# Where the head norms' sums and spreads stand among the steps of two gated linear units

## The reference, cut to what matters

```python
o_a = _norm_f32(o_a) * jax.nn.silu(heads(rg))
o_b = _norm_f32(o_b) * gdn_norm_w * jax.nn.silu(heads(bg))
o_c = _norm_f32(o_c) * gla_norm_w * jax.nn.silu(heads(cg))
o_d = _norm_f32(o_d) * hgrn_norm_w * jax.nn.silu(heads(dg))
o = jnp.concatenate([o_a, o_b, o_c, o_d], axis=-1)
return jnp.matmul(o, w_out)

def _norm_f32(x):
    return x * lax.rsqrt(jnp.mean(x * x, axis=-1, keepdims=True) + EPS)
```

## Time and profile before

| | |
|---|---|
| median of three runs | 2418.09 us |
| the profiled execution | 2420.88 us, of which its span is 2419.1 us |
| mean granted TensorE clock | 0.973 of full |
| busy share of TensorE, VectorE, ScalarE, POOL | 97%, 68%, 27%, 8% |
| uses 15 to 28 of the mixers | about 324 to 368 us of the span |

### The profile page before, as it was taken

The page is one execution under the profiler, slowest core; times in us unless marked ns, Lnnn a source line. Parts: engine busy times, 40 slices in busy tenths (PEclk is TensorE's granted clock), DMA queues, the critical chain, the costliest instruction groups (busy, mean ns, idle before and its releaser), DMA issues.

```text
span 2419.1 us, 35289 instructions
## 1 busy us (share of the span) xinstructions
PE 2335.3 (97%) x14624; PEld 1898.2 (78%) x14624; DVE 1651.3 (68%) x2569; ACT 663.9 (27%) x1200; POOL 183.2 (8%) x179
## 2 busy tenths in 40 slices
PE   8998879999999999999989999999999999999997
PEld 6886668878888888887756788888888888888886
DVE  6674366756888865559788777666667886666653
ACT  2321253022211201324768413222102113222200
POOL 0001222001000011003211010000010000000000
PEclk9999579999999999999999999999999999999998
DMA  4220003412222453322200361232562451322341
GB/s 183 79 79 2 21 3 122 158 52 88 96 96 96 135 204 130 107 81 92 88 1 2 138 219 62 98 100 97 197 214 104 182 186 63 102 96 96 127 141 64
DMA packets 71728, 253.94 MB, mean 105 GB/s; under 512 B 8560, under 2 KB 8848, under 8 KB 71056
## 3 DMA queue, kind: packets, MB, share of 16 engines
q1 hardware_dynamic: 71280, 251.14, 30.4%
q10 hardware_dynamic: 288, 0.54, 0.1%
HBM read 247.97 MB, written 2.10 MB: 103 GB/s over the span
## 4 chain that ended last, share of the span: by engine, by line
PE 47%; DVE 3%; issue 0%; ACT 0%; POOL 0%; DVEq 0%; POOLq 0%
PE psum L393 14%; PE psum L394 14%; PE psum L395 13%; PE psum L3362 1%; PE psum L487 1%; PE psum L3349 1%; PE psum L3384 1%; DVE scratch L3440 1%; DVE scratch L3416 1%; PE psum L656 0%; PE psum L3376 0%; PE psum L465 0%; DVE h L534 0%; DVE n L530 0%; PE psum L476 0%
## 5 line engine op out<-in xcount | busy, mean ns | idle before, releaser
L393 PE MATMUL psum<-rounded_n,rounded_high 128*128 128x512 f32 x1824 | 722.1, 396 | 8.0 <-DVE rounded_ring L346 4.6
L394 PE MATMUL psum<-rounded_n_low,rounded_high 128*128 128x512 f32 x1824 | 712.1, 390 | 0.0
L395 PE MATMUL psum<-rounded_n,rounded_ring 128*128 128x512 f32 x1824 | 712.0, 390 | 0.0
L346 DVE TENSOR_TENSOR rounded_ring<-ring,rounded_high 128x1024 fp32r<-128x1024 f32 (+1 forms) x360 | 448.4, 1246 | 43.5 <-ACT rounded_high L329 31.5
L393 PEld LDWEIGHTS psum<-rounded_n,rounded_high 128*128 128x128 f32 x1824 | 343.9, 189 | 86.6 <-issue 7.4
L394 PEld LDWEIGHTS psum<-rounded_n_low,rounded_high 128*128 128x128 f32 x1824 | 344.1, 189 | 74.2 <-issue 3.9
L395 PEld LDWEIGHTS psum<-rounded_n,rounded_ring 128*128 128x128 f32 x1824 | 343.7, 188 | 72.1
L344 DVE CAST rounded_high<-ring 128x1024 fp32r<-128x1024 f32 (+1 forms) x347 | 250.4, 722 | 188.3 <-PE psum L395 177.9
L393 PE MATMUL psum<-rounded_arena,rounded_high 128*128 128x512 f32 x720 | 280.2, 389 | 0.0
L395 PE MATMUL psum<-rounded_arena,rounded_ring 128*128 128x512 f32 x720 | 280.1, 389 | 0.0
L394 PE MATMUL psum<-rounded_arena,rounded_high 128*128 128x512 f32 x720 | 280.1, 389 | 0.0
(11 more groups left out here) (507 smaller groups left out, 2798.3 us busy)
## 6 DMA issues: line engine op xcount, KB each, us to landing
ring<-in_w_up SPq DMA_DIRECT2D x132, 512.0 KB, 3.6
ring<-in_w_down SPq DMA_DIRECT2D x48, 512.0 KB, 3.5
n_low<-in_mod_w SPq DMA_DIRECT2D x48, 512.0 KB, 5.8
arena<-in_mod_w SPq DMA_DIRECT2D x48, 512.0 KB, 5.3
ring<-in_w_ab_in SPq DMA_DIRECT2D x37, 512.0 KB, 3.6
ring<-in_w_mix_in SPq DMA_DIRECT2D x31, 512.0 KB, 3.6
ring<-in_w_sc_in SPq DMA_DIRECT2D x24, 512.0 KB, 5.7
ring<-in_w_down SPq DMA_DIRECT2D x24, 384.0 KB, 3.0
```

What stands on the lines that cost most here:

```text
L346: nc.vector.tensor_tensor(self.rounded(raw), raw, self.rounded(high), ALU.subtract).then_inc(self.weights_split, 1)
L393: self.nc.tensor.matmul(out, w_high, x_high, start=first, stop=False)
L394: self.nc.tensor.matmul(out, w_high, x_low, start=False, stop=False)
L395: return self.nc.tensor.matmul(out, w_low, x_high, start=False, stop=last)
```

## The change

Sums, spreads, values, casts and low parts of tiles 0 to 5 are put at other places of the three hand-written lists. No instruction of them is added or dropped.

```diff
@@ TensorE @@
         use(14)
-        for i in range(4):
-            norm_sums(pe, i)
+        norm_sums(pe, 0)
         use(15)
+        norm_sums(pe, 1)
         use(16)
-        for i in range(3):
-            norm_spread(pe, i)
         use(17)
+        norm_sums(pe, 2)
         use(18)
-        norm_spread(pe, 3)
+        norm_sums(pe, 3)
         use(19)
         use(20)
-        for i in (4, 5):
-            norm_sums(pe, i)
+        norm_spread(pe, 0)
         use(21)
+        norm_spread(pe, 1)
         use(22)
+        norm_spread(pe, 2)
+        use(23)
+        norm_spread(pe, 3)
+        use(24)
+        norm_sums(pe, 4)
+        use(25)
+        norm_sums(pe, 5)
+        use(26)
+        use(27)
         for i in (4, 5):
             norm_spread(pe, i)
-        for x in range(23, len(uses)):
-            use(x)
+        use(28)
@@ ScalarE @@
-        norm_root(0)
-        after_use(15)
-        after_use(16)
+        for x in range(15, 19):
+            after_use(x)
         act.wait_ge(delta_kept, 2)
         for i in (4, 5):
             square(i)
-        after_use(17)
-        after_use(18)
-        for i in range(2):
+        norm_root(0)
+        for x in range(19, 22):
+            after_use(x)
+        high_part(0)
+        for i in (1, 2, 3):
+            after_use(21 + i)
             high_part(i)
-        after_use(19)
-        after_use(20)
-        for i in (2, 3):
-            high_part(i)
+        after_use(25)
+        after_use(26)
         norm_root(1)
-        for x in range(21, 25):
-            after_use(x)
+        after_use(27)
         for i in (4, 5):
             high_part(i)
-        for x in range(25, len(uses)):
-            after_use(x)
+        after_use(28)
@@ VectorE @@
         use(15)
-        norm_scale(0)
         use(16)
         k.split_until(dve, k.first_tile["mix_out"] + 1)
-        use(17)
-        norm_value(0)
-        norm_value(1)
-        use(18)
-        norm_value(2)
-        use(19)
-        norm_value(3)
-        low_part(0)
-        low_part(1)
+        for x in (17, 18, 19):
+            use(x)
+        norm_scale(0)
         use(20)
         dve.wait_ge(delta_kept, 2)
         for i in (4, 5):
             gate(i)
+        norm_value(0)
         use(21)
-        low_part(2)
-        low_part(3)
-        norm_scale(1)
+        norm_value(1)
         use(22)
         k.split_until(dve, k.first_tile["mix_out"] + 2)
+        low_part(0)
+        norm_value(2)
         use(23)
-        norm_value(4)
-        norm_value(5)
-        for x in range(24, 26):
-            use(x)
+        low_part(1)
+        norm_value(3)
+        use(24)
+        low_part(2)
+        use(25)
+        low_part(3)
+        use(26)
+        norm_scale(1)
+        use(27)
+        for i in (4, 5):
+            norm_value(i)
         for i in (4, 5):
             low_part(i)
-        for x in range(26, len(uses)):
-            use(x)
+        use(28)
```

## The result

The change makes the kernel slower. Six executions of the changed kernel have a median of 2429.53 us (2422.54 to 2431.47), six of the kernel before one of 2417.47 (2414.76 to 2421.79). The ratio is 1.0033 with a 95% interval of 1.0018 to 1.0049. A second set of eleven executions gave 1.0034 (1.0020 to 1.0049), so this is no accident of one set. The forecast was no change, 2420.8, with a range up to 2425.2; the result lies above it. The profiled execution took 2431.02 us with a span of 2429.2.

The account below looks back on a forecast made before the run. The prediction took the kernel as bound by TensorE (busy 97%), and the stage by when use 28 starts and how long it lasts. Terms -0.5 + 4.2 - 1.0 = +2.7 us on median 2418.09 gave 2420.8, range 2416.2 to 2425.2.

Parts of the forecast that it names:

- Part 1: End of unit 1: moving sums of tiles 1 to 3 from ahead of use 15 gains 2.6 to 3.2 us.
- Rival C: TensorE at full clock from use 16 to the end of use 28: -0.65 us, 2417.4; chance 0.13.
- Part 2: Unit 1's end to pair 15: ScalarE's root with two table loads takes 4.75 us, leaving 0.9 to 1.5 gained.
- rival E: Each table load keeps ScalarE for as long again, 1.28 us: +6.5 us in all, 2424.6; chance 0.02.
- Part 3: VectorE from pair 15 to use 24: 0.7 us longer; use 24 still starts 0.5 us earlier than before.
- Part 4: Use 24 to use 28: added sums, root wait ahead of pair 20 and spreads cost 4.2 us (2.8 to 5.1).
- rival B: TensorE at half clock from use 24 after a pause: 7.6 us against 4.57, total +6.9, 2425.0; chance 0.17.
- Part 5: Use 28, mostly at full clock, takes 5.3 us instead of 6.35: a gain of 1.0.
- Rival D: Only VectorE's stretch counts, something as late covers the reciprocal's wait: about -2.5 us, 2415.6; chance 0.08.

Follow-up runs that it names:

- e11: Changed kernel with sums 0 to 3 in one piece ahead of use 15, as before the change; median 2426.10 us, ratio 1.0028 to the kernel before.
- e3: Kernel before with only the pieces of tiles 4 and 5 moved to where the change has them; median 2422.90 us, ratio 1.0022.
- e7: Kernel before with matmuls that compute nothing used, 6 behind use 26 and 4 behind BIG; median 2415.53 us, ratio 0.9993.
- e9: Kernel before, unedited, run again for a second trace; median 2419.90 us, ratio 1.0000.
- e12: e6 with sums 0 to 3 in one piece ahead of use 15; median 2412.99 us, ratio 0.9977 to the kernel before.
- e1: Changed kernel with VectorE's reciprocal of tiles 4 and 5 behind pair 20 instead of ahead of it; median 2426.05 us, ratio 1.0032.
- e2: Changed kernel with tiles 4 and 5 earlier: sums behind spread 0, reciprocal ahead of use 22, spreads ahead of use 27; median 2424.95 us, ratio 1.0017.
- e5: Changed kernel with nothing of tiles 4 and 5 between use 24 and use 28; median 2418.96 us, ratio 1.0005 to the kernel before.
- e6: Changed kernel with one later root for tiles 0 to 5, VectorE's norm values and low parts behind use 24, spreads re-placed; median 2414.99 us, ratio 0.9981.
- e8: Changed kernel, unedited, run again for a second trace; median 2428.78 us, ratio 1.0034 to the kernel before.
- e10: Changed kernel with 8 matmuls that compute nothing used, behind spread 3 and ahead of use 24; median 2427.87 us, ratio 1.0033.

## Why the prediction was wrong, point by point

- **Part 1**, sums one by one: 2.0 us won at pair 13, 2.6 to 3.2 at the unit's end. Pair 11 to the unit's end fell by 2.52 between the first two traces, so the arithmetic came out, though by e11 only 0.70 of it are the sums themselves. The premise did not hold: the half clock in which the old piece of sums takes 7 us is not there in every execution. Over the six traces with the piece (before, e3, e7, e9, e11, e12) three ran at full clock, 13.4, and three at half, 15.8 and 17.6. (The three at full are e3, e7 and e9 on two chips; e11 and e12 are from the third, and the chip of the first trace isn't on record, so chance and chip are not separated here.) In the seven with distributed sums and no matmuls to fill the pause (changed, e1, e2, e5, e6, e8, e10) it was 15.06 or 15.07 each time. The range of this part should have reached to a loss of 1.7. Rival C's argument "half clock with as much work" took the same trace for a rule.
- **Part 2**, two tables ahead of pair 15: 4.75 us forecast, 4.75 measured, and 1.77 where e6 took them out. No drain as in rival E: the root starts 0.02 us behind the load's end (339.99 + 1.28, 341.29).
- **Part 3**, VectorE's stretch: +0.7 forecast, +0.67 measured. One reading in it was wrong: TensorE's pauses between the uses there were 1.56 and 1.68 us in the first trace, not longer than a spread at half clock (1.85). It cost nothing that the trace shows, since the profile lists no wait of VectorE between pair 15 and use 24 in the changed kernel.
- **Part 4 is the step that failed.** Its structure was right: VectorE waits for the root ahead of pair 20 (4.51 us), the spreads end last ahead of use 28. The failing step is "TensorE, full clock: ... = 4.57 us". It was 7.85. I had this as rival B with a price of 7.6 and a chance of 0.17. What I held against B was that use 24 ran fast before after a pause. That pause was 1.42 us, and the one that the change makes is 4.02; e5 and e10 show that with work in it use 24 runs at full clock (1.15 us). The Trainium skill (TensorE: Matmul & The Clock Gate, "What's actually happening") says that the throttled state is the default, that activity releases it and that idleness brings it back. The traces agree in kind (clock 1.00 ahead of the pause, 0.50 behind it); the prediction named this only for the hopeful case. I could have worked the new pause out from my own parts 1 to 3: spread 3 had to end some 3 us ahead of use 24, as rival B itself says. With 7.85 in place of 4.57 my lower and upper sums for this part would be 14.4 and 16.7 against 8.30; it took 15.9.
- **Part 5**, use 28: 5.3 taken, 4.6 as the bound; 4.55 measured.
- **The sum.** In the first pair of traces the stage lost 5.6 us, rival B's mechanism, whose sum was +6.9. Against e9 it lost 10.0. By those two the loss is between, and the means of the executions say 8. The top of the range, 2425.2, stood just above B's 2425.0, and both on a median of three executions and on one trace of a kernel whose first stretch goes two ways. The rest of the miss is probably that base: with the 4.4 us of e9's faster stage added, B's time would have reached 2429.4. That is an estimate; how often each state of that stretch comes is not known.
- **Rival D** fell: nothing covered the root.

## What to carry to other kernels

A pause made longer by moving work out of it can cost more than the work did: count TensorE's pauses in the new order, not only its chain, and price what follows a longer one at the slow clock as well. A wait put ahead of a small instruction costs what hangs on that instruction; late norm pieces belong behind the last step that the chain needs, as in e5 and e6, and a table switch belongs where its engine has slack. Before a part is priced on a stretch at half clock, a second trace of the same kernel is worth more than any arithmetic on the first.

## What the runs showed of the hardware

Two executions of one kernel can differ by 4.4 us in a single stage with the same instructions; 4.2 of them lie in the first stretch, where the granted clock was 0.50 in the sums of one and 0.98 in those of the other. Both traces of the changed kernel lose 1.3 to 1.4 us behind the stage against both of the kernel before (2052.1 twice against 2050.8 and 2050.7), where no instruction differs. Windows of 1030 to 1100 us, the kernel before and then the changed one:

```profile
1030.00:1100.00 70.00, 70.00 (x387) 58.31 (x386) 41.42 (x73) 19.37 (x26) 5.18 (x3) 0.93 0.27 84
```

```profile
1030.00:1100.00 70.00, 70.00 (x380) 58.72 (x379) 33.55 (x61) 18.45 (x25) 0.00 (x0) 0.90 0.26 82
```

The mean clock there is 0.93 and 0.90, by the rounded means some 3 to 6 us more at 1.2 GHz. In e5 and e11 it went the other way: 1.00 in this window, and 2046.9 and 2047.0 us behind the stage. Over all fourteen traces what lies behind the stage took 2046.9 to 2052.4 us, so a few us between two kernels' times can't be put down to the edited stage without a look at the rest. That the edit's shift in time is what moves this clock is not shown, and that such shifts are steady for a kernel rests on two traces of each.
